# Reordering VectorE's work within a pair of the up projection

## What is computed

```
h = rms_norm(x, norm2_g)
u = causal_dwconv(h @ w_up, ffn_conv_w)      # w_up: 1024 x 6144, 3 taps per channel
gate, up = split(u, 2)
x = x + (gelu(gate) * up) @ w_down
```

## Time and profile before

| | |
|---|---|
| median of 3 runs | 1745.59 us (1745.45 to 1747.6) |
| profiled execution | 1745.45 us |
| its span | 1743.6 us |
| TensorE busy | 1700.4 us, 98% |
| VectorE busy | 1228.0 us, 70% |
| ScalarE busy | 794.3 us, 46% |
| GpSimd busy | 518.3 us, 30% |

### The profile page before, as it was taken

How to read it: one execution, slowest core, us unless ns; L and a number is a source line. 1 busy time by engine, 2 the same in 40 slices (tenths; PEclk the granted TensorE clock), 3 DMA queues, 4 the chain that set the end, 5 groups by cost and what they waited for, 6 DMA issues and landing times.

```text
span 1743.6 us, 20915 instructions
## 1 busy us (share of the span) xinstructions
PE 1700.4 (98%) x7556; PEld 1380.7 (79%) x7556; DVE 1228.0 (70%) x1442; ACT 794.3 (46%) x1038; POOL 518.3 (30%) x284
## 2 busy tenths in 40 slices
PE   7999999999999999999999999998999999999998
PEld 6888878888787888888888788877778877666686
DVE  6577771369999888888888789876456545666654
ACT  5466641235754343434434445442422255666631
POOL 4221222200026456545541000014333331444320
PEclk8999999999999999999999999998999999999999
DMA  8111112152412322322224957641411320110251
GB/s 256 49 36 48 48 36 73 37 205 85 169 49 85 96 72 84 96 72 76 89 65 154 349 192 234 207 128 48 133 48 61 97 73 13 37 49 25 102 212 73
DMA packets 161095, 176.96 MB, mean 101 GB/s; under 512 B 13566, under 2 KB 114692, under 8 KB 161028
## 3 DMA queue, kind: packets, MB, share of 16 engines
q1 hardware_dynamic: 158724, 167.67, 30.0%
q10 hardware_dynamic: 2304, 8.39, 1.3%
HBM read 140.38 MB, written 35.65 MB: 101 GB/s over the span
## 4 chain that ended last, share of the span: by engine, by line
PE 84%; DVE 9%; ACT 3%; DMA 2%; issue 1%; POOL 1%; SPq 0%; POOLq 0%; DVEq 0%; ACTq 0%
PE ps L916 28%; PE ps L2375 23%; PE ps L2329 17%; PE ps L2596 4%; PE ps L2566 3%; PE ps L2581 3%; PE ps L2626 2%; PE ps L2569 2%; PE ps L2568 1%; DVE lat L2092 1%; DVE hop_lo_P L1802 1%; PE ps L2553 1%; POOL z_lo L1010 1%; DVE square_dve L1619 0%; DMA dn_raw<-gu_park 0%
## 5 line engine op out<-in xcount | busy, mean ns | idle before, releaser
L940 POOL TENSOR_TENSOR w_lo<-w_raw,w_hi 128x1024 fp32r<-128x1024 f32 x52 | 135.9, 2615 | 626.1 <-ACT w_hi L1039 626.1
L2375 PE MATMUL ps<-hop_hi_P,wop_hi_P 128*128 128x512 f32 x672 | 262.5, 391 | 4.7 <-DVE u L1836 3.3
L2375 PE MATMUL ps<-hop_hi_P,wop_lo_P 128*128 128x512 f32 x672 | 261.5, 389 | 0.0
L2375 PE MATMUL ps<-hop_lo_P,wop_hi_P 128*128 128x512 f32 x672 | 261.5, 389 | 0.0
L916 PE MATMUL ps<-h_hi,w_hi 128*128 128x512 f32 x752 | 235.8, 395 | 11.8 <-DVE h_lo L1604 8.3
L946 POOL TENSOR_TENSOR wop_lo_P<-pair_sum,wop_hi_P 128x512 fp32r<-128x512 f32 x90 | 136.6, 1517 | 354.5 <-ACT wop_hi_P L1050 354.5
L916 PE MATMUL ps<-h_lo,w_hi 128*128 128x512 f32 x752 | 233.8, 392 | 0.0
L916 PE MATMUL ps<-h_hi,w_lo 128*128 128x512 f32 x752 | 233.8, 392 | 0.0
L916 PEld LDWEIGHTS ps<-h_hi,w_hi 128*128 128x128 f32 x752 | 142.3, 190 | 43.5 <-issue 14.4
L916 PEld LDWEIGHTS ps<-h_lo,w_hi 128*128 128x128 f32 x752 | 142.6, 190 | 30.1
L916 PEld LDWEIGHTS ps<-h_hi,w_lo 128*128 128x128 f32 x752 | 142.6, 190 | 30.1
(11 more groups left out here) (350 smaller groups left out, 3367.6 us busy)
## 6 DMA issues: line engine op xcount, KB each, us to landing
pair_raw<-in_w_up SPq DMA_DIRECT2D x48, 512.0 KB, 4.8
w_raw<-in_w_in SPq DMA_DIRECT2D x46, 512.0 KB, 3.9
dn_raw<-gu_park SPq DMA_DIRECT2D x84, 256.0 KB, 3.8
dn_raw<-in_w_down SPq DMA_DIRECT2D x60, 256.0 KB, 3.0
gu_park<-up_cv SPq DMA_DIRECT2D x24, 512.0 KB, 2.6
out_raw<-in_w_out SPq DMA_DIRECT2D x30, 256.0 KB, 2.8
x_tok<-in_x SPq DMA_DIRECT2D x4, 1024.0 KB, 8.0
x_park<-xs SPq DMA_DIRECT2D x1, 4096.0 KB, 14.3
```

What stands on the lines that cost most here:

```text
L940: nc.gpsimd.tensor_tensor(lo[:, :], raw[:, :], hi[:, :].bitcast(f32), ALU.subtract).then_inc(w_lo_done, 1)
L2375: mm = nc.tensor.matmul(dst, w[q][:, k, :], x[q][:, k, :], start=a, stop=b, skip_group_check=True)
```

## The change

Within a period VectorE's instructions get another order; none is added or taken away, and the other engines' lists stay as they are.
- `gate_up(k)` goes from period k+1, behind U3(k+1) and C22(k+1), to the end of period k, ahead of them. (For pair 23 it was at the end already.)
- The four sums for pair k+2 were s1 behind the gate scale, s2 and s3 behind the up taps, and s4 in period k+1 behind `gate_up(k)`. They become s1 and s2 behind the gate scale, s3 and s4 behind the up taps.
- The gate taps go ahead of C12 and the up scale.
- In period 0, s1 and s2 for pair 2 go from behind the two scales to behind both pairs of taps, together with s3 and s4, and `gate_up(0)` follows.

```
             def first_period():
                 k = Pair(0, 0)
                 scale(k, "gate")
-                pair_sums(k.plus(2), (0,))
                 dve.wait_ge(product, nth("P3", k))
                 V.tensor_tensor(bank(k, "c"), bank(k, "c"), u2[0][:, :], ALU.add).then_inc(sums_done, 1)
                 scale(k, "up")
-                pair_sums(k.plus(2), (1,))
                 third_sums(k.plus(1))
                 taps(k, 0)
                 taps(k, 1)
-                pair_sums(k.plus(2), (2, 3))
+                pair_sums(k.plus(2), range(4))
+                gate_up(k)
...
             def period(k):
                 if not the(k, 1):
                     third_sums(k)
-                if not the(k, 0):
-                    gate_up(k.plus(-1))
-                if not the(k, 0) and not the(k, 1) and known(k, 1):
-                    pair_sums(k.plus(1), (3,))
...
                 scale(k, "gate")
                 if known(k, 2):
-                    pair_sums(k.plus(2), (0,))
+                    pair_sums(k.plus(2), (0, 1))
+                taps(k, 0)
                 dve.wait_ge(product, nth("P3", k))
                 V.tensor_tensor(bank(k, "c"), bank(k, "c"), u2[k.par][:, :], ALU.add).then_inc(sums_done, 1)
...
                 scale(k, "up")
-                taps(k, 0)
...
                 if known(k, 1):
                     second_sum(k.plus(1))
                 taps(k, 1)
                 if known(k, 2):
-                    pair_sums(k.plus(2), (1, 2))
-                if the(k, PAIRS - 1):
-                    gate_up(k)
+                    pair_sums(k.plus(2), (2, 3))
+                gate_up(k)
```

More of the change, by code:

```diff
@@ L1951, in period @@
                     third_sums(k)
[L1952 to L1955, removed]
                 if the(k, 0):
```

## The result

The changed kernel takes 1788.18 us (median of 4 runs, 1786.17 to 1789.61) against 1745.59 us (4 runs). The ratio is 1.0241, with an interval of 1.0223 to 1.0259: slower by 42.6 us. The prediction said 1783.7 us, 38.2 more. The profiled execution took 1788.3 us, with a span of 1786.5 us, 42.9 more than the 1743.6 of before.

What follows compares the result with a forecast made beforehand. The prediction took TensorE's unbroken matmuls, 19.05 us a period, as the bound. It summed 5.9 + 33.4 - 1.1 = 38.2 us onto 1745.45 us to give 1783.7 us, with a range of 1759 to 1793 (central case 1776 to 1792).

Steps and rivals of the forecast that it cites:

- The mechanism: Regular periods: s3, s4 and `gate_up` take turns with three GpSimd low parts, delaying U3; TensorE stops about 1.6 us before P4.
- The steady term, 33.4: Regular periods, pair 2 to pair 22: 20 intervals each 1.67 us longer, 33.4 us in all.
- the 1.67 of a period: Regular period: C21 to C21 takes 20.72 us instead of 19.05, 1.67 us more.
- the step of U3: Regular period's tail: U3(k+1) comes 16.94 us after C21 instead of 13.61, once `gate_up` has ended.
- The move costs nothing: Regular period: gate taps ahead of C12 put U2 at 8.45 us, needed only at 10.7, with 2.2 us of cover.
- the 11.86: Regular period: the up taps end 11.86 us after C21, when s3 is ready.
- less than 1.8 late: Regular periods: no steady loss if U3 is less than 1.8 us late; the no-loss rival, 1747.5 us, chance 0.07.
- The start, 5.9: First periods: P4(2) starts at 546.2 instead of 540.35, 5.9 us lost by then.
- The end, -1.1: Last pair: with `gate_up(22)` out of the way, C21(23) comes 1.1 us earlier, a gain of 1.1.
- and `gate_up(23)` follows: Last pair: `gate_up(23)`, its transfer and the loads behind it follow C21(23), which comes 1.1 us earlier.
- The clock: Rival: TensorE's stops of 1.7 us per period bring a fall to 1.2 GHz, far above the range; chance 2%.
- The rival's sign: Clock rival, chance 2%: TensorE's clock falls to 1.2 GHz with its stops of 1.7 us in each period.

Runs made afterwards that it cites:

- The undoings: The changed kernel with one part put back: `gate_up` 1751.62 us, s4 1752.71 us, the gate taps 1749.66 us.
- the write-only kernel: The changed kernel with GpSimd's low parts subtracting one column per block and writing zeros to the rest: 1747.59 us, 1.0012.
- the run with the taps back: The changed kernel with the gate taps back behind the up scale, sums and `gate_up` as changed: 1749.66 us, 1.0014.
- The kernel with only the ends changed: The kernel before with `gate_up(0)` moved behind the up taps of pair 1 and `gate_up(22)` to the end of period 22: 1742.55 us, 0.998.
- the kernel with the gate taps alone: The kernel before with only the gate taps moved ahead of C12: 1747.93 us, 1.0012.
- those with `gate_up`, s4 and the taps back: The changed kernel with `gate_up`, s4 or the gate taps each put back by itself: 1751.62, 1752.71 and 1749.66 us.
- the one with the start undone: The changed kernel with s1 and s2 of pair 2 back behind the two scales of period 0: 1788.41 us, 1.0249.
- s3 early: The changed kernel with s3 also behind the gate scale, only s4 and `gate_up` at the end: 1764.4 us, 1.0103.

## Why the prediction held, point by point

**The mechanism: right.** The stops stand where it put them, once a period, 1.55 us ahead of P4 and released by U3; `gate_up` takes 2.31 and s4 1.78 us; P7's low part gets its turn ahead of `gate_up`, as closely as foreseen (its cast ends at 14.31 after C21 and s4 at 14.87); the P6 cast no longer waits in the regular periods. The undoings and the write-only kernel bear out that it is the tail with its turns.

**The steady term, 33.4: measured 36.07.** The mis-sized term is the 1.67 of a period, in the step of U3 and in what follows it: U3 at 17.02 and not 16.94 (0.08), P4 0.82 behind it and not 0.74 (0.08), C21 3.06 behind P4 and not 3.04 (0.02). That is 1.85 a period for 1.67. The full 20 x 1.85 would be 37.0, and it is not reached because the last two intervals are shorter: eighteen intervals of C21 are 20.89 in the mean (550.05 to 926.07), and those behind them 20.45 and 20.47. There the up taps end 11.44 after C21 instead of 12.05, and U3 stands at 16.62 and 16.64; why is open.

**"The move costs nothing" (the gate taps): half right.** For U2 and P7 it is so, and alone in the kernel before it costs 0.3 to 3.8 us, none of it in the regular periods. But the prediction counted its cover only up to the next product. The same move shifts the end of the up taps, and so the whole tail, by 1.1 us, and on top of the other two moves this is enough for U3 to lose its cover, as the run with the taps back shows. The sum had it in (the 11.86), but the words put the cost elsewhere.

**The point from which it decides, "less than 1.8 late": near.** 13.61 + 1.8 is 15.4; by the table it is 15.16 (19.04 - 3.88).

**The start, 5.9: measured 5.96.** C21(1) came 0.26 later than worked out, when both are counted from C21(0), P7(2) 0.26 and P4(2) 0.1. The table load is on the path as foreseen, for the first gelu waits behind it:

```profile
524.03 0.62 ACT L1050 CAST wop_hi_P<-pair_sum 128x512 fp32r<-128x512 f32 x1 [7.51 <-DVE pair_sum L1825]
524.67 1.28 ACT L1378 ACT_TABLE_LOAD   x1
525.96 1.06 ACT L1378 ACTIVATE gate_cv<-gate_cv 128x1024 f32<-128x1024 f32 x1
```

**The end, -1.1: measured -0.24.** C21(23) did come 3.07 behind P4(23) instead of 4.13, which is the 1.06. The step that failed is "and `gate_up(23)` follows". The gate taps now stand ahead of C12, and come so early behind the gate scale that they wait for ScalarE:

```profile
984.40 0.70 DVE L1836 TENSOR_TENSOR ps<-ps,s1c 128x512 f32<-128x512 f32 x1
...
986.21 1.23 DVE L1911 TENSOR_TENSOR ps<-ps,xs 128x1024 f32<-128x1024 f32 x1
988.62 2.60 DVE L1608 SCALAR_TENSOR_TENSOR gate_cv<-ps,vec,gate_cv 128x1023 f32<-128x1023 f32 x2 [1.18 <-ACT gate_cv L1353]
...
998.05 1.23 DVE L1945 TENSOR_TENSOR up_cv<-gate_cv,up_cv 128x1024 f32<-128x1024 f32 x1
```

From C21(23) to `gate_up(23)` it is now 13.65 us, where before it was 12.28 (942.55 to 954.83); counted from P4(23) it is 16.72 instead of 16.41. The kernel with only the ends changed keeps the old order of the taps, has the 12.28 again (939.78 to 952.06), and keeps its gain. So the reading of the end was right for `gate_up(22)`; what was not costed are the gate taps of pair 23, which have no sums ahead of them to cover ScalarE's 1.2 us.

**The clock.** I gave 2% to a fall that would go on through all periods, and there is none: the granted clock of the regular periods is 1.00. But there was a short one, behind the stop ahead of P7(2), the longest of the stage: some eight matmuls ran at the 1.2 GHz level, 0.43 us apart:

```profile
537.98 0.51 PE L2369 MATMUL ps<-hop_hi_P,wop_hi_P 128*128 128x512 f32 x1 [2.75 <-DVE u L1836]
...
538.71 0.63 PE L2369 MATMUL ps<-hop_hi_P,wop_lo_P 128*128 128x512 f32 x1
539.14 0.63 PE L2369 MATMUL ps<-hop_hi_P,wop_hi_P 128*128 128x512 f32 x1
...
547.01 0.49 PE L2369 MATMUL ps<-hop_hi_P,wop_hi_P 128*128 128x512 f32 x1 [1.70 <-DVE u L1836]
```

The granted clock between 538 and 541 us is 0.56. It cost nothing here, since P4(2) waits 1.70 us for U3(2) all the same. By what the prediction cites on this from the Trainium skill, stops of this length are too short for a fall; the trace shows one behind 2.75 us, and the measurement decides. The rival's sign, a fall that lasts, did not come, but this reason against it does not hold.

**What stays open.** What the start costs by itself was not measured, for its undoing brought on a slow stretch of its own. Why the clock is low for 28 matmuls ahead of 500 us in some executions and for 12 in others was not looked into either.

## What to carry to other kernels

An engine's slack belongs to the period, not to one instruction: a move that is free alone may be the one that uses up the cover, so add up all moves that end in the same wait and compare the sum with the one cover they share. Where two engines take turns, ask of each moved instruction whom it now meets, not only what it waits for. And the irregular periods at both ends are worth their own reading: here they held the only gain, 2.8 us, while the regular ones could only lose.

## What the runs showed of the hardware

- **Turns between VectorE and GpSimd.** Where VectorE (two inputs in SBUF) and GpSimd (reading SBUF) both have work queued, they take strict turns: a 128x1024 product takes 2.31 us instead of 1.22, a 128x512 sum 1.78 instead of 0.69, and GpSimd's 128x512 subtraction up to 2.34 instead of 1.29 (at 674.22 in the kernel with the gate taps alone). Beside a write-only memset none of it appears.
- **The clock behind a single stop.** In five traces a stop of 2.71 to 2.75 us had six to eight matmuls 0.43 us apart behind it (the changed kernel, those with `gate_up`, s4 and the taps back, and the one with the start undone). Behind a stop of 4.44 us (s3 early) there were ten. Behind other stops, of 1.2 to 1.9 us and one of 2.49 us, there were none. But the length of the stop does not decide it: in the write-only kernel the stop was 1.94 us, TensorE started again at the full rate, and seven matmuls 0.43 us apart began 1.56 us later:

```profile
536.52 0.50 PE L2370 MATMUL ps<-hop_hi_P,wop_hi_P 128*128 128x512 f32 x1 [1.94 <-DVE u L1837]
...
537.56 0.39 PE L2370 MATMUL ps<-hop_lo_P,wop_hi_P 128*128 128x512 f32 x1
...
538.08 0.63 PE L2370 MATMUL ps<-hop_hi_P,wop_hi_P 128*128 128x512 f32 x1
```

The price is about 1.6 us for eight (0.2 us each), and it depends on what comes next whether it is felt: it was hidden in the changed kernel, ahead of a product that waits anyway, and paid in full in P4(2) of the kernel with the start undone. It was also paid in the kernels with `gate_up` or the taps back and in the write-only one, where P4(2) waits for nothing: there C21(2) comes 10.1 us after P7(2)'s first matmul, where it was 8.49 (534.79 to 543.28).
